# A hybrid decoder layer on one core: half of the output projection inside attention, later key queries inside the expert loop, and each expert row's diagonal made by ScalarE

## The chip, the cores and the metric

The kernel runs on 1 core of a Trainium2 chip. The metric is the device time of one execution in microseconds (us); the median of three runs is 1033.25 (1033.0 to 1033.98). Engines: TensorE (PE, matmuls; PEld its weight loads), VectorE (DVE), ScalarE (ACT), GpSimd (POOL) and SyncE (SP), which here only issues DMAs.

## The reference

Input x is 256 tokens of 1024 float32. One layer does this:

```python
z, xbc, dt, q, kvs, gate = split(h @ w_in)
y_ssd = rms_norm(ssd_scan(conv(xbc), dt) * silu(z))           # in 2 groups of 512
y_att = rms_norm(sparse_attention(q, kvs, gate))              # 16 heads, 3 branches
mix   = concatenate([y_ssd, y_att], -1) @ w_out
h     = layer_norm(ALPHA * h + mix)
# PEER: product-key retrieval, 8 heads, 16 experts of 16384 per head and token
s     = (h @ w_query) against sub_keys;  top 16 of each half, top 16 of their 256 sums
g     = softmax(chosen scores);  e = chosen expert numbers
a     = gelu(dot(h, expert_u[e]))
ffn   = sum over the 128 (head, k) of  g * a * expert_v[e]
out   = layer_norm(ALPHA * h + ffn)
```

The learned weight of rms_norm multiplies on, the scale of a token is one number per token.

## The kernel before, in words

Tokens stand on the 128 partitions, in two tiles (i = 0, 1). The program has a serial part and a loop.

Serial part: input projections of both tiles, convolution, SSD scan of both tiles, then attention of tile 0 (function calls `scores`, `maxima`, `exps`, `weights`, `weight_transposes`, `weight_copy`, `values`, in steps u of two heads, three ahead), its output projection (`mixer_transposes`, `mix_part`), residual and first layer norm, transposes of h (`hidden_transposes`), queries (`query_part`, `query_transposes`, `key_scores`) and the choice of the experts of head 0 (`choose`, all VectorE).

Loop: 256 rows, `g`, 128 per tile and 16 per head (`u = g // 16`, `k = g % 16`). For each row GpSimd gathers per partition one 8 KB line, the expert's u and v (1 MB in all), into a ring of 8 slots (10 from row `SWITCH` on, when the weights' buffers are free). VectorE dots its u half with h (L1514), ScalarE takes the gelu, VectorE multiplies the identity by gelu and gate into one of four diagonal matrices (`weigh`, L1486, one row later: `LAG`), and TensorE multiplies the diagonal by the v half, adding into two banks (`weighted`, L923, which signals `row_used` for GpSimd). VectorE also chooses the experts of the next head, in parts after rows 1 to 7 of a head.

Into the rows of tile 0, tile 1's attention, projection, norm and queries are threaded. A table written by hand (`step_tables`) says after which row each engine issues which piece; each engine runs its own list in order, and semaphores join them. SyncE brings 2 MB pieces of weights into two buffers, each asked for when the piece two before is used up; they share the DMA engines with the gathers. `bank_plan` deals the eight PSUM banks to the pieces in the same order.

## Time and profile before

| | us |
|---|---|
| median of three runs | 1033.25 |
| the profiled execution | 1033.95 |
| its span, first to last instruction | 1032.1 |
| busy: TensorE, weight loads | 890.0, 445.6 |
| busy: VectorE, ScalarE, GpSimd | 664.8, 267.7, 312.0 |
| mean granted TensorE clock | 0.969 |
| read from memory | 333.50 MB, of it 268.45 MB gathers |

Busy time is the sum of an engine's instructions, and says nothing of whether anyone waited for them. The DMA share is the mean busy share of the core's 16 DMA engines. "Idle before <-X" is the time in which an engine stood still ahead of an instruction, and what released it. A clock of 1.0 is TensorE's 2.4 GHz level, 0.5 its 1.2 GHz level; a value between is a mean over both.

### The profile page before, as it was taken

How to read it: one execution, taken by the hardware profiler on the slowest of the kernel's cores; microseconds unless marked ns; L12 is line 12 of the kernel's file. 1: busy time of each engine (PE TensorE's matmuls, PEld its weight loads, DVE VectorE, ACT ScalarE, POOL GpSimd, SP SyncE). 2: the span in 40 equal slices, each digit the busy share in tenths (PEclk: the TensorE clock that was granted, in tenths of full speed). 3: DMA queues.
4: the chain of work that ended last, by engine and by line, in shares of the span. 5: the costliest groups of instructions: out<-in, count | busy, mean ns of one | idle time of the engine just before them, and what ended most of it. 6: DMA issues, size and time to landing. Idle time of an engine off the chain costs nothing.

```text
span 1032.1 us, 8596 instructions
## 1 busy us (share of the span) xinstructions
PE 890.0 (86%) x2666; PEld 445.6 (43%) x2666; DVE 664.8 (64%) x1654; ACT 267.7 (26%) x665; POOL 312.0 (30%) x294
## 2 busy tenths in 40 slices
PE   7999998859788998998999888889888787877875
PEld 6876546546354343444544333344333222222221
DVE  2512005851243998989977685859879788788755
ACT  1121125373022555554321121113112011021000
POOL 0020001200030443443533343343535543444420
PEclk9999999989899898999999998989999999999998
DMA  6343664002659898999999999999999999999991
GB/s 252 147 140 141 231 263 174 1 1 82 244 208 423 340 422 326 407 388 377 396 421 423 422 421 422 421 422 399 399 421 421 421 421 422 420 422 421 420 422 64
DMA packets 44477, 335.11 MB, mean 325 GB/s; under 512 B 5904, under 2 KB 5904, under 8 KB 7824
## 3 DMA queue, kind: packets, MB, share of 16 engines
q0 software_dynamic: 36864, 268.45, 63.5%
q1 hardware_dynamic: 7568, 66.12, 16.4%
q8 instruction: 21, 0.34, 0.1%
q14 instruction: 24, 0.20, 0.0%
HBM read 333.50 MB, written 1.05 MB: 324 GB/s over the span
## 4 chain that ended last, share of the span: by engine, by line
PE 35%; DVE 23%; DMA 23%; issue 11%; ACT 7%; POOL 1%; DVEq 0%; SPq 0%; POOLq 0%; ACTq 0%
DMA late<-in_uv,eidx 11%; PE ps L649 8%; PE ps L923 7%; PE ps L641 6%; DMA ring<-in_uv,eidx 5%; DMA wring<-in_uv,eidx 5%; PE ps L784 5%; PE ps L758 4%; ACT L967 3%; DVE late L1514 3%; DVE late L1486 3%; ACT tmp L967 3%; DVE ring L1514 3%; DVE late L1194 2%; DMA wring<-in_wts 1%
## 5 line engine op out<-in xcount | busy, mean ns | idle before, releaser
L923 PE MATMUL ps<-late 128*128 128x512 f32 x480 | 233.2, 617 | 42.1 <-DVE late L1486 41.5
L923 PE MATMUL ps<-ring,late 128*128 128x512 f32 x480 | 234.7, 623 | 40.1 <-DVE late L1486 39.8
L1610 POOL DMA_INDIRECT late<-in_uv,eidx x120 | 134.6, 1122 | 294.6 <-PE ps L923 191.0
L1610 POOL DMA_INDIRECT ring<-in_uv,eidx x120 | 140.1, 1168 | 183.2 <-PE ps L923 179.8
L967 ACT ACTIVATE late<-late 128x1 f32<-128x1 f32 (+2 forms) x275 | 58.7, 218 | 511.2 <-DVE late L1514 510.4
L1514 DVE CUSTOM_DVE_ANT_0 late<-late,x_sb 128x1024 f32<-128x1024 f32 x120 | 146.7, 1223 | 56.6 <-DMA late<-in_uv,eidx 55.1
L1514 DVE CUSTOM_DVE_ANT_0 ring<-ring,x_sb 128x1024 f32<-128x1024 f32 x120 | 146.7, 1222 | 55.5 <-DMA ring<-in_uv,eidx 53.4
L923 PEld LDWEIGHTS ps<-ring,late 128*128 128x128 f32 x480 | 87.9, 196 | 162.5 <-DVE late L1486 83.2
L923 PEld LDWEIGHTS ps<-late 128*128 128x128 f32 x480 | 86.6, 194 | 163.7 <-DVE late L1486 88.0
L967 ACT ACT_TABLE_LOAD x84 | 107.8, 1283 | 14.5 <-PE ps L641 13.0
L1486 DVE TENSOR_SCALAR late<-cst,late 128x128 f32<-128x128 f32 x256 | 88.0, 344 | 26.7 <-ACT late L967 26.6
L649 PE MATMUL ps<-wring,tmp 128*128 128x347 f32 (+4 forms) x256 | 84.6, 492 | 0.0
L967 ACT ACTIVATE tmp<-ps 128x512 f32<-128x512 f32 (+3 forms) x88 | 44.4, 513 | 86.5 <-PE ps L641 41.2
L641 PE MATMUL ps<-tmp,wring 128*128 128x256 f32 x256 | 58.0, 391 | 6.7 <-DMA wring<-in_wts 6.7
L649 PEld LDWEIGHTS ps<-wring,tmp 128*128 128x128 f32 x256 | 48.5, 189 | 35.5 <-issue 14.8
L784 PE MATMUL ps<-wring,tmp 128*128 128x512 f32 (+1 forms) x144 | 58.8, 558 | 0.7 <-issue 0.7
L641 PEld LDWEIGHTS ps<-tmp,wring 128*128 128x128 f32 x256 | 50.4, 197 | 13.9 <-DMA wring<-in_wts 6.7
L923 PE MATMUL ps<-wring,late 128*128 128x512 f32 x64 | 31.4, 615 | 10.4 <-DVE late L1486 10.3
L784 PEld LDWEIGHTS ps<-wring,tmp 128*128 128x128 f32 x144 | 28.1, 198 | 27.6 <-issue 25.4
L1233 DVE TENSOR_SCALAR dtb<-dtb 128x32 f32<-128x32 f32 x1 | 0.2, 181 | 58.8 <-ACT dtb L967 58.8
L967 ACT ACTIVATE late<-ps 128x512 f32<-128x512 f32 (+4 forms) x22 | 11.5, 524 | 79.7 <-PE ps L649 74.2
L1584 POOL TENSOR_TENSOR tmp<-late,cst 128x128 f32<-128x128 f32 x4 | 1.8, 452 | 91.6 <-PE ps L659 91.4
(198 smaller groups left out, 822.7 us busy)
## 6 DMA issues: line engine op xcount, KB each, us to landing
wring<-in_wts SPq DMA_DIRECT2D x23, 2048.0 KB, 10.1
wring<-in_wts SPq DMA_DIRECT2D x2, 1428.0 KB, 5.7
wring<-in_wts SPq DMA_DIRECT2D x2, 1388.0 KB, 5.6
wring<-in_wts SPq DMA_DIRECT2D x4, 512.0 KB, 7.4
lnw<-in_ln SPq DMA_DIRECT2D x4, 512.0 KB
late<-in_uv,eidx POOLq DMA_INDIRECT x120
ring<-in_uv,eidx POOLq DMA_INDIRECT x120
wring<-in_wts SPq DMA_DIRECT2D x1, 1432.0 KB, 7.3
```

The costliest lines, as they stand in the source:

```text
L641: last = mm(o[:, 0:T], w[:, c % 4, k, :], xT_sb[:, k, :], start=k == 0, stop=k == KD - 1)
L649: last = mm(o[:, 0:width], xT_sb[:, k, i * P:(i + 1) * P], w[:, k, :], start=k == 0, stop=k == KD - 1)
L758: last = mm(mix[half], mixTs[i][n][:, c, :], mix[2][:, c, half * 512:(half + 1) * 512], start=m + c == 0, stop=n + c == 6)
L784: last = mm(o[:, 0:heads * 256], hTails[i][:, k, :], w[:, k, first * 256:(first + heads) * 256], start=k == 0, stop=k == KD - 1)
L923: last = mm(o[n], diag[:, g % DIAGS, :], v_row[:, n * 512:(n + 1) * 512], start=False, stop=False, skip_group_check=True)
L967: return nc.scalar.activation(out, in_, func, **kw)
L1194: return V.tensor_tensor(out, a, b, op)
L1233: link(V.tensor_scalar(dtb[:, 4, :, :], dtb[:, 2, :, :], 1.0, None, ALU.add))
L1486: V.tensor_scalar(diag[:, g % DIAGS, :], ident, wact[:, e, 0, k:k + 1], gate[:, e, k:k + 1], ALU.mult, ALU.mult).then_inc(diag_ready, 1)
L1514: V.tensor_tensor_reduce(out=u_row, in0=u_row, in1=h_sb[:, i, :], scale=1.0, scalar=0.0, op0=ALU.mult, op1=ALU.add, accum_out=hdot[:, e, k ...
L1584: G.tensor_tensor(krt[:, :, 0:HD // 2], src[:, :, HD // 2:HD], bc(ksin[:, 0:HD // 2], 1, NKV), ALU.mult)
L1610: G.indirect_dma_start(row(slots[g]), None, uv, bass.IndirectOffsetOnAxis(eidx[:, u % 2, k:k + 1], 0)).then_inc(row_here[slots[g]], 16)
```

## The change

It has five parts. (1) The gate multiply of the SSD output moves to the end of each tile's SSD scan, the squares of both tiles to the start of attention. TensorE transposes tile 0's SSD half at u = -1 and does its share of the output projection in eight slices, one after `values` of each step, into banks of its own (`mixS`); the attention half goes into `mixA`, and its rms scale, one number per token, is applied in the residual instead of ahead of the transposes. (2) Residual, layer norm and last output work in halves of 512 columns. (3) Only the queries of heads 0 to 3 stay ahead of row 0; heads 4 to 7 follow in the loop at rows 14, 25, 36 and 47 (`EARLY`). (4) `choose` has 15 small parts instead of 7, spread over rows 16u - 23 to 16u - 9; `SWITCH` is 160. (5) ScalarE makes gate times gelu and the diagonal, both as copies with a scale; the lag of a row is gone, as are the two matmul pairs with zeros that opened and closed a sum.

```diff
-SWITCH = 176
+SWITCH = 160
-LAG = 1
+EARLY = 3
...
+    for n, k in enumerate((14, 25, 36, 47)):
+        queries(0, EARLY + n, k, 1, 3)
...
# tensor
             for u in range(-AHEAD, NU[0] + 1):
...
+                if u == -1:
+                    mixer_transposes(0, 0)
                 if u >= 1:
                     values(0, u - 1)
+                    c = u - 1
+                    mix_blocks(0, c // 4, by_block[c % 4 * 2:c % 4 * 2 + 2])
...
-            mixer_transposes(0, 0)
-            for m in range(4):
-                mix_part(0, m)
             mixer_transposes(0, 1)
             for m in range(4, 8):
                 mix_part(0, m)
             hidden_transposes(0)
-            for n in range(len(QUERIES[0])):
+            for n in range(EARLY):
...
# scalar, in the loop
                 f(wact[:, e, 0, k:k + 1], hdot[:, e, k:k + 1], ACT.Gelu).then_inc(w_step, 1)
+                if k == 0:
+                    act.wait_ge(gate_ready, u + 1)
+                act.wait_ge(w_step, g + 1)
+                f(wact[:, e, 1, k:k + 1], wact[:, e, 0, k:k + 1], ACT.Copy, scale=gate[:, e, k:k + 1]).then_inc(gw_step, 1)
+                act.wait_ge(gw_step, g + 1)
+                if g >= DIAGS:
+                    act.wait_ge(row_used, g - DIAGS + 1)
+                f(diag[:, g % DIAGS, :], ident, ACT.Copy, scale=wact[:, e, 1, k:k + 1]).then_inc(diag_ready, 1)
...
# vector
-            def weigh(g):
-                dve.wait_ge(w_step, g + 1)
-                if g >= DIAGS:
-                    dve.wait_ge(row_used, g - DIAGS + 1)
-                V.tensor_scalar(diag[:, g % DIAGS, :], ident, wact[:, e, 0, k:k + 1], gate[:, e, k:k + 1], ALU.mult, ALU.mult).then_inc(diag_ready, 1)
...
+            def residual(i, half):
+                if half == 0:
+                    dve.wait_ge(sd_ready, 2 * i + 2)
+                    link(V.reciprocal(st[:, 12:13], st[:, 20:21]))
+                o = await_full(dve, "mixA", i, half)
+                cols = slice(half * 512, (half + 1) * 512)
+                taken(V.scalar_tensor_tensor(r1s[i][:, cols], o, st[:, 12:13], x_sb[:, i, cols], ALU.mult, ALU.add), "mixA", i, half)
+                await_taken(dve, "mixA", i, half)
+                statistics(r1s[i], half, 24)
+            def layer_norm(dst, src, scratch, at, value, ln_value, part, ready):
+                if part == 0:
+                    dve.wait_ge(ln_here, ln_value)
+                    for half in range(2):
+                        cols = slice(half * 512, (half + 1) * 512)
+                        last = V.scalar_tensor_tensor(scratch[:, cols], src[:, cols], bna[:, 0:1], lnw[:, 0, cols], ALU.subtract, ALU.mult)
+                    link(last)
+                else:
+                    dve.wait_ge(sd_ready, value)
+                    link(V.reciprocal(st[:, at:at + 1], st[:, at + 8:at + 9]))
+                    for half in range(2):
+                        cols = slice(half * 512, (half + 1) * 512)
+                        V.scalar_tensor_tensor(dst[:, cols], scratch[:, cols], st[:, at:at + 1], lnw[:, 1, cols], ALU.mult, ALU.add).then_inc(ready, 1)
```

TensorE before, from the last steps of tile 0's attention on (L867 transposes of the weights, L880 and L889 values, L746 transposes for the projection, L758 the projection, L769 transposes of h):

```order
L867 MATMUL ps<-cst,tmp 128x128 x4
L880 MATMUL ps<-late,tmp 128x256
L889 MATMUL ps<-late,tmp 128x64 x8
L746 MATMUL ps<-cst,s_all 128x128 x8
L758 MATMUL ps<-wring,late 128x512 x16
L746 MATMUL ps<-cst,s_all 128x128 x8
L758 MATMUL ps<-wring,late 128x512 x16
L769 MATMUL ps<-cst,x_sb 128x128 x8
```

TensorE after, at the same place (L896, L909 and L918, L767, L778 and L798 are those lines' new numbers):

```order
L896 MATMUL ps<-cst,tmp 128x128 x4
L909 MATMUL ps<-late,tmp 128x256
L918 MATMUL ps<-late,tmp 128x64 x4
L778 MATMUL ps<-wring,late 128x512 x2
L918 MATMUL ps<-late,tmp 128x64 x4
L778 MATMUL ps<-wring,late 128x512 x2
L767 MATMUL ps<-cst,s_all 128x128 x8
L778 MATMUL ps<-wring,late 128x512 x16
L798 MATMUL ps<-cst,x_sb 128x128 x8
```

The first projection of 16 matmuls is gone from behind the last values, and pairs of its matmuls stand behind the values of each step instead.

ScalarE before, near row 5 to 10 of the loop (late 128x1 is the gelu, tmp,lsum the exponentials of tile 1's attention; their table loads stand between):

```order
L967 ACT_TABLE_LOAD
L967 ACTIVATE tmp,lsum<-ps,nmx 128x256 x2
L967 ACT_TABLE_LOAD
L967 ACTIVATE late<-late 128x1 x3
L967 ACT_TABLE_LOAD
L967 ACTIVATE tmp,lsum<-ps,nmx 128x256 x2
L967 ACT_TABLE_LOAD
L967 ACTIVATE late<-late 128x1 x3
L967 ACTIVATE tmp<-ps 128x512
L967 ACTIVATE late<-late 128x1
L967 ACTIVATE tmp<-ps 128x512
```

ScalarE after, at the same place (late<-late 128x1 x2 is a gelu and the product with the gate, late<-cst,late the diagonal):

```order
L992 ACT_TABLE_LOAD
L992 ACTIVATE tmp,lsum<-ps,nmx 128x256 x2
L992 ACT_TABLE_LOAD
L992 ACTIVATE late<-late 128x1 x2
L992 ACTIVATE late<-cst,late 128x128
L992 ACTIVATE late<-late 128x1 x2
L992 ACTIVATE late<-cst,late 128x128
L992 ACTIVATE late<-late 128x1 x2
L992 ACTIVATE late<-cst,late 128x128
```

Every gelu is followed by its product and its diagonal, and the exponentials of a unit stand between the diagonals of two rows.

TensorE after, inside the loop where the first late query stands (L953 a row's matmuls, L813 the query's, L888 and L889 scores, L909 and L918 values of tile 1); before, no L784 stands among the rows ahead of row 98:

```order
L953 MATMUL ps<-ring,late 128x512 x4
L909 MATMUL ps<-late,tmp 128x256
L918 MATMUL ps<-late,tmp 128x64 x4
L813 MATMUL ps<-wring,tmp 128x256 x4
L953 MATMUL ps<-ring,late 128x512 x2
L888 MATMUL ps<-kT,tmp 128x512
L889 MATMUL ps<-cmask_h,ident_h 128x2x128
L813 MATMUL ps<-wring,tmp 128x256 x4
L953 MATMUL ps<-late 128x512 x2
```

The query's 8 matmuls come in two parts of four between the rows.

## Rows read from the trace of the kernel before

**Rows 1.** Busy us (xcount) per engine by stretch; granted clock, DMA share, GB/s.

```profile
196.93:241.04 44.11, 30.64 (x174) 23.26 (x173) 21.91 (x53) 29.73 (x98) 7.19 (x12) 0.88 0.00 1
299.55:329.72 30.17, 25.04 (x84) 12.12 (x83) 5.00 (x15) 6.95 (x12) 8.21 (x8) 1.00 0.95 390
329.72:499.71 169.99, 161.19 (x513) 77.22 (x513) 151.08 (x398) 88.68 (x190) 71.01 (x60) 0.95 0.95 378
499.71:740.00 240.29, 216.41 (x528) 95.23 (x526) 184.32 (x470) 46.83 (x126) 95.50 (x84) 0.96 1.01 416
740.00:1008.00 268.00, 210.97 (x450) 77.97 (x451) 209.65 (x533) 40.85 (x133) 118.31 (x104) 1.00 1.01 421
```

**Rows 2.** GpSimd in order: start, duration, gather [idle before <-releaser].

```profile
299.55 1.14 POOL L1610 DMA_INDIRECT late<-in_uv,eidx  x1 [93.75 <-DVE eidx L1394]
...
329.72 1.48 POOL L1610 DMA_INDIRECT late<-in_uv,eidx  x1 [19.83 <-PE ps L923]
```

**Rows 3.** TensorE in order, from attention of tile 0 to the queries.

```profile
208.76 0.63 PE L867 MATMUL ps<-cst,tmp 128*128 128x128 f32 x4 [3.77 <-ACT tmp L967]
...
241.04 1.04 PE L746 MATMUL ps<-cst,s_all 128*128 128x128 f32 x8
...
258.56 13.97 PE L758 MATMUL ps<-wring,late 128*128 128x512 f32 x32 [0.44 <-DVE late L1194]
...
281.70 5.26 PE L784 MATMUL ps<-wring,tmp 128*128 128x256 f32 x16 [0.73 <-issue]
...
288.92 3.62 PE L784 MATMUL ps<-wring,tmp 128*128 128x256 f32 x16
...
303.60 1.13 PE L801 MATMUL ps<-sk,tmp 128*128 128x128 f32 x8 [0.73 <-issue]
```

**Rows 4.** VectorE in order: residual, layer norm, dot of row 0.

```profile
271.78 1.48 DVE L1339 SCALAR_TENSOR_TENSOR late<-x_sb,ps 128x512 f32<-128x512 f32 x2 [12.63 <-PE ps L758]
...
277.72 1.22 DVE L1194 TENSOR_TENSOR x_sb<-late,lnw 128x1024 f32<-128x1024 f32 x1
...
305.37 1.23 DVE L1514 CUSTOM_DVE_ANT_0 late<-late,x_sb 128x1024 f32<-128x1024 f32 x1 [5.77 <-DMA late<-in_uv,eidx]
```

**Rows 5.** DMA issues of the page: xcount, KB each, us to landing.

```profile
wring<-in_wts SPq DMA_DIRECT2D x23, 2048.0 KB, 10.1
```

**Rows 6.** Groups in 329.72 to 499.71: busy, mean ns, idle before <-releaser.

```profile
L923 PE MATMUL ps<-ring,late 128*128 128x512 f32 x118 | 58.6, 624 | 5.8 <-DVE late L1486 5.8
...
L1486 DVE TENSOR_SCALAR late<-cst,late 128x128 f32<-128x128 f32 x61 | 21.1, 345 | 14.6 <-ACT late L967 14.6
```

**Rows 7.** ScalarE's groups in 329.72 to 499.71.

```profile
L967 ACT ACT_TABLE_LOAD x40 | 51.3, 1283 | 0.7
...
L967 ACT ACTIVATE late<-late 128x1 f32<-128x1 f32 x61 | 11.4, 200 | 82.2 <-DVE late L1514 81.8
L967 ACT ACTIVATE tmp<-ps 128x512 f32<-128x512 f32 x16 | 9.3, 579 | 0.0
```

**Rows 8.** ScalarE's 128x128 group in attention of tile 0.

```profile
L967 ACT ACTIVATE tmp<-ps,nmx 128x128 f32<-128x128 f32 x32 | 11.3, 382 | 3.1 <-DVE nmx L1429 3.0
```

**Rows 9.** ScalarE in order inside the loop.

```profile
409.79 0.58 ACT L967 ACTIVATE tmp<-ps 128x512 f32<-128x512 f32 x1
410.39 1.28 ACT L967 ACT_TABLE_LOAD   x1
411.69 0.47 ACT L967 ACTIVATE tmp<-ps,nmx 128x256 f32<-128x256 f32 x1
```

**Rows 10.** All engines in order, the tail.

```profile
1015.42 1.23 DVE L1514 CUSTOM_DVE_ANT_0 ring<-ring,x_sb 128x1024 f32<-128x1024 f32 x1 [0.98 <-DMA ring<-in_uv,eidx]
...
1016.97 3.70 PE L923 MATMUL ps<-ring,late 128*128 128x512 f32 x8 [0.49 <-DVE late L1486]
...
1021.57 0.69 DVE L1492 SCALAR_TENSOR_TENSOR tmp<-x_sb,ps 128x512 f32<-128x512 f32 x1 [4.29 <-PE ps L960]
...
1028.76 0.34 SPq L616 DMA_DIRECT2D out<-tmp  x1
```

More of the change, by code:

```diff
@@ L97, in step_tables @@
     put("pe", 8, "pcT")
[L98 removed]
+    put("act", 11, "pcT")
     for u in range(NU[1]):
@@ L135, in step_tables, with queries @@
-    for n, k in enumerate((130, 131, 133, 134, 137, 138, 139)):
-        put("dve", k, "finish", n)
-    put("act", 135, "root2")
-    return at
+    def queries(i, n, k, gap, copy):
+        for part in range(2):
+            put("pe", k + part * gap, "q", i, n, part)
+        k += gap
+        put("act", k + copy, "q", i, n)
+        put("pe", k + copy + 1, "qpT", i, n)
+        put("act", k + 2 * copy + 1, "qpT", i, n)
+        put("pe", k + 2 * copy + 2, "s", i, n)
+        put("act", k + 3 * copy + 2, "s", i, n)
@@ new lines, in step_tables @@
+    for n, k in enumerate((14, 25, 36, 47)):
+        queries(0, EARLY + n, k, 1, 3)
+    put("pe", 60, "mT", 0)
+    put("dve", 63, "mT", 0)
+    for part, k in enumerate((64, 67, 69, 71)):
+        put("pe", k, "mix", part)
+    put("dve", 70, "taken")
+    put("act", 71, "squares")
+    put("pe", 72, "mT", 1)
+    put("dve", 73, "mean")
+    put("act", 74, "root", 12, 4)
+    for half in range(2):
+        put("dve", 74 + half, "partial", half)
+    put("dve", 76, "mT", 1)
+    for part, k in enumerate((77, 79, 81, 83)):
+        put("pe", k, "mix", 4 + part)
@@ new lines, in step_tables, with choice_step @@
+    put("dve", 85, "residual", 0)
+    put("dve", 87, "residual", 1)
+    put("act", 88, "root", 24, 5)
+    put("dve", 88, "norm", 0)
+    put("dve", 89, "norm", 1)
+    put("pe", 90, "hT")
+    put("act", 93, "hT")
+    queries(1, 0, 94, 2, 3)
+    queries(1, 1, 108, 4, 4)
+    queries(1, 2, 126, 4, 4)
+    queries(1, 3, 144, 4, 4)
+    for part, k in enumerate((132, 133, 135, 136)):
+        put("dve", k, "finish", part)
+    put("act", 134, "root", 36, 6)
+    return at
+def choice_step(u, part):
+    if u == 1:
+        return part // 2
+    if u == PH:
+        return TOPK * u - 21 + max(part - 2, 0)
+    return TOPK * u - 23 + part
@@ L554, in layer @@
         for i in range(NT):
-            order += [(14 + n, 3 * i + n + 1 if n < 3 else ("mix", i, 1)) for n in range(4)]
+            order += [(14 + n, (2 * i + 1, ("mixS", i, 1), 2 * i + 2, ("mixA", i, 1))[n]) for n in range(4)]
             order += [(18 + n, ("q", i, max(g for g, group in enumerate(QUERIES[i]) if group[0] == n))) for n in range(4)]
@@ L913, in _ @@
             hidden_transposes(0)
-            for n in range(len(QUERIES[0])):
+            for n in range(EARLY):
                 query_part(0, n, 0, 1)
@@ L931, in _ @@
                 o = [await_free(pe, "y", i, n) for n in range(2)]
-                for n in range(2):
-                    mm(o[n], zero, nothing, start=True, stop=False, skip_group_check=True)
                 for g in range(STEPS * i, STEPS * (i + 1)):
                     weighted(g, o)
-                    for what, n in items_at["pe"][g]:
+                    for what, *n in items_at["pe"][g]:
                         if what == "compressed":
@@ L1124, in _ @@
             token_copies(0)
+            for i in range(NT):
+                ssd_squares(i)
             compressed_exp(0)
+            root(0, 2 * NG, 1)
             for u in range(-AHEAD, NU[0]):
@@ L1464, in _ @@
                     maxima(0, u + AHEAD)
-                if u in GATE_AT:
-                    ssd_gate(GATE_AT.index(u))
-                if u - 1 in GATE_AT:
-                    ssd_norm(GATE_AT.index(u - 1))
+                if u == 0:
+                    mixer_transposed(0, 0)
+                if u == 1:
+                    ssd_norm(1)
             attention_taken(0)
-            mixer_transposed(0, 0)
+            mixer_transposed(0, 1)
+            for half in range(2):
+                partial(0, half)
```

412 lines of the change are left out of this document (180 added, 232 removed).

## The prediction

> **What bounds the kernel now.** Read first the busy time by stretch [rows 1]: mean GB/s and DMA share there say where the memory queue is full. From 499.71 us on it is: 416 GB/s, then 421, at a DMA share of 1.01. That is the ceiling of this loop; each of its 256 rows is a 1 MB gather (2.49 us at 421 GB/s), and nothing that an engine saves there moves the end. Three parts lie outside that ceiling. Before 299.55 us the gathers have not begun. From 299.55 to 329.72 (390 GB/s) and on to 499.71 (378 GB/s) the queue has gaps: the two stretches moved 30.17 x 390 + 169.99 x 378 = 76,020 KB (GB/s times us), which at 421 are 180.6 us, but took 200.2. So 19.6 us are lost there. Last comes the tail behind the last row.
>
> Next, GpSimd's own rows [rows 2]. Eight gathers go out from 299.55, when the first indices are ready; the ninth waits 19.83 us for TensorE and goes at 329.72. From there to the 69th at 499.71, where I cut the stretch, there are 60 rows (x60 for GpSimd in its row, [rows 1]) in 170.0 us, 2.83 us each, slower than the queue. In that stretch TensorE is busy 161.19 of 169.99 us at a clock of 0.95, VectorE 151.08, ScalarE 88.68: TensorE is the nearest to a bound, with VectorE close behind, and the ring starts it 20 us in arrears.
>
> Then the path to 299.55 on TensorE and VectorE [rows 3, 4]. Attention of the first tile ends at 241.04; behind it stand in a row the output projection of the SSD half and that of the attention half, 13.97 us each with transposes ahead (the second, from 258.56, stands for both), residual and layer norm, transposes, and queries from 281.70. In 196.93 to 241.04 TensorE worked only 30.64 of 44.11 us [rows 1].
>
> **The change, part by part.**
>
> *First gather.* The SSD half of the projection (16 matmuls, 13.97 us) and its 8 transposes (1.04 us) move into attention. TensorE's work there becomes 30.64 + 13.97 + 1.04 = 45.65 us, more than the 44.11 us the stretch has now, so TensorE becomes its bound. Some idle time stays: the first weights to be transposed appear at 208.76, after a wait of 3.77 and a shorter one; I keep 5 us. The clock, 0.88 on average in this stretch, should be nearer to full without the later pauses; I take 2 us back (of at most 30.64 x 0.12 = 3.7). The gate multiply of tile 0 (a 1024-wide VectorE operation, 1.22 us by [rows 4]) now stands in the SSD stage ahead of the second tile's work and delays the start by 1.2. End of attention with its mixing: 196.93 + 1.2 + 45.65 - 2 + 5 = 246.8. Transposes of the attention half: 1.2 with the first copy behind them, so the projection runs 248.0 to 262.0; its scale is applied only in the residual, hence no norm ahead of it. VectorE then does half a residual (0.74), its statistics (as wide, 0.7), small ones (0.4), two half-width multiplies (1.3), a reciprocal and two more (1.5): 4.8 with gaps, to 266.8. One transposing group and its copy remain: 268.1, where queries start, against 281.70. The choice behind it has the same instructions. So the first gather moves by 13.6, to 286.0. Were all the old idle time (13.5) to stay, it would be 294; with 2 us of idle and the whole clock, 281. A 2 MB piece of weights lands in 10.1 us at the median [rows 5]; the last of w_out is asked for when the SSD half is done (246.8) and needed 7 us into the attention half, at 255: this could cost 2, which is inside these bounds.
>
> *First 60 rows.* Queries of heads 4 to 7 leave the stretch ahead of row 0. TensorE is free at 304.73 - 13.6 = 291.1 [rows 3]; row 0 is dotted 5.8 us after its issue, as now, at 291.8. Then dot 1.3, three ScalarE operations 0.9, two matmuls 2.0: row 0 is used at 296.0 and the ninth gather goes at 296.1, 10.1 us after the first instead of 30.2. The ring no longer runs dry at the start. What those queries cost inside the loop: four groups of one head, each 8 matmuls of 256 columns (3.62 by [rows 3]) with transposes and scores, about 4.3 together: 17.2 us on TensorE, in rows 14 to 60. The stretch for 60 rows is then 161.19 + 17.2 = 178.4 plus idle. Idle was 8.8, 5.8 of it waits for VectorE's diagonal before the one kind of row alone [rows 6]. VectorE loses 60 x 0.34 us of diagonals and 14.6 us of waits for ScalarE, and can run ahead by as many rows as the ring holds, so I take half, 4.5 (bounds 0 and 20). The 69th gather goes at 296.1 + 183 = 479.1. The same 180.6 us of transfers lie ahead of it, so the gaps are 479.1 - 286.0 - 180.6 = 12.5 us instead of 19.6: 7.1 gained. With no idle and the clock full (161.19 x 0.95 + 17.2 = 170) they are 0 by this sum; 3 stay for the first landing. With 20 of idle they are 28.
>
> *ScalarE.* No operation of it in the trace multiplies by a per-row scalar onto 128 columns. The nearest row is the 128x128 exponential with a pointer bias, 382 ns; above it stands 579 for 512 columns and below it 200 for one column [rows 7, 8]. I take 0.38, and 0.20 for the product of gate and activation, as for the gelu. Each waits for the one before it. Per row: 0.20 + 0.38 and 0.08 of handing over more than now. In the stretch: 88.68 + 60 x 0.66 + 12 copies x 0.38 = 133 us of 183. It fits on average. It also shortens the path from a row's landing to its use by most of a row, since VectorE made each diagonal one row late; beyond row 68 the full queue hides that, and it shows in the tail alone. The copies need no table: in the row at 409.79 a copy runs between a gelu and the load for exp [rows 9], and the list of instructions has 80 loads against 84.
>
> The Trainium skill (ScalarE: Activation LUTs, What ACT_TABLE_LOAD costs) says that a switch costs a load of about 1283 ns and a drain of about 1380 ns behind it. The load agrees; the drain does not show here: the load at 410.39 is followed by the exponential at 411.69, 1.30 us on.
>
> *Finer choice, earlier tenth slot.* The same instructions in fifteen parts; indices of the next head are ready at the same rows (16u - 10, and row 118 for head 8). Where the queue is full this is worth nothing; if heads were late it would show at row 128, and 499.71 to 740 loses only 240.3 x 5/421 = 2.9 us. The ring of ten from row 160 instead of 176 lies in that full queue: nothing.
>
> *Tail.* Now: last dot at 1015.42, the matmuls of the last two rows from 1016.97 (3.70), a closing matmul pair, first residual at 1021.57, output issued at 1028.76 [rows 10]. After: dot 1.2, ScalarE 0.9, one row's matmuls 2.0, so the residual starts 4.2 us after the dot instead of 6.15; from there 2.8 for residual and statistics, 0.5 small ones, 1.3 and 1.5 for the norm with the last half issued 6.2 later instead of 7.2, and half a transfer, 0.3 less. Together 3.2 gained (bounds 2 and 4).
>
> **Sum**, against the profiled execution's own 1033.95 us (span 1032.1): -13.6 - 7.1 - 3.2 = -23.9, so 1010.0; the median of the runs lies 0.7 lower, hence **1009.3**, say 1009.
>
> **Rivals.**
> *The queue never starves after the first row.* For: eight rows of lead are kept, and VectorE is relieved. Against: 178 us of TensorE work for 60 rows is more than their 149 us of gathers, and close to the 180.6 of all transfers. Gaps 3 instead of 12.5: 1000.
> *ScalarE is late now and then.* Its order is fixed: a unit of attention puts two table loads (2.57) and two exponentials between two rows' diagonals, and four diagonals are all the lead it has. For: VectorE already waited 14.6 us there for gelus behind such loads [rows 6], and now TensorE stands directly behind them. Against: 73% busy. With 20 us of idle on TensorE: 1025. If every one of the 40 loads of the stretch [rows 7] cost 1.38 more, ScalarE's own work would be 188 us, the stretch 5 longer than TensorE's 183 and with its waits 9: 1018. That is what the drain of the Trainium skill's rule (same page and section) would do; the rows speak against it.
> *TensorE stays as interrupted in attention as before.* The first gather at 294 instead of 286: 1017.
> *Slower than before.* ScalarE becomes the bound of the first 60 rows: a diagonal waits for a slot that TensorE frees, TensorE for a value unit's copy that stands behind that diagonal. The gain of 24 us is used up when 60 rows take 183 + 24 = 207 us, 3.45 each; ScalarE's work is 2.2 of it, so 1.25 of waiting per row is the turning point. At 3.6 per row the time is 1042. Against: the copies stand three steps behind the matmuls they need.
>
> **How the numbers follow.** A difference under 0.2% (2 us) can't be told from none. Forecast 60%, with its own range 1003 to 1015; never starving 17%; ScalarE late 10%; the drain 2%; attention as before 5%; slower 5%; everything cancelling out 1%. The range goes from below the case without starvation with an early first gather (281: -5) and a tenth cut off, to between attention as before and ScalarE late: 997 to 1021. Faster 0.94, same 0.01, slower 0.05.
>
> **What would show it.** First gather at 286 (281 to 290) and ninth within 11 us of it; TensorE busy over 43 us from 197 to 247; the 69th gather at 479 and about 390 GB/s between; from there 416 to 421 as before; no more waits of VectorE on ScalarE; the operation with 128 columns on ScalarE at 0.38; residual 4.2 us behind the last dot. I am wrong if TensorE's waits for ScalarE's diagonal in these 60 rows pass 10 us, if the first gather is later than 290, or if the full queue after row 68 falls below 415.

## The result, and the profile after

The changed kernel takes **1006.07 us** (median of 4 runs, 1003.62 to 1006.71) against 1033.62 us (1033.0 to 1035.21, 4 runs) before: 0.9727 of it, 95% interval 0.9707 to 0.9747. 1009 was predicted, with 997 to 1021 as the range. The profiled execution of the changed kernel took 1003.62 us with a span of 1001.8; it is the fastest of the four, 2.5 us under their median, so the traces differ by 30.3 us where the medians differ by 27.6.

First the busy times by stretch, in the columns of [rows 1]. Cuts are at the first gather (287.51), the ninth (299.85), the 69th (473.81), rows 128 and 200, and the start of the last dot (988.57):

```profile
196.93:247.97 51.04, 44.81 (x225) 29.27 (x225) 25.14 (x57) 29.86 (x99) 7.25 (x12) 0.97 0.13 46
...
287.51:299.85 12.34, 7.80 (x23) 3.48 (x21) 2.51 (x9) 3.98 (x7) 8.04 (x9) 0.79 0.85 335
299.85:473.81 173.96, 172.90 (x597) 92.63 (x597) 140.12 (x360) 132.33 (x327) 65.97 (x61) 0.96 1.00 408
473.81:654.43 180.62, 161.59 (x397) 71.52 (x396) 114.00 (x274) 75.95 (x211) 65.89 (x61) 0.95 1.01 422
654.43:828.82 174.39, 149.04 (x343) 59.30 (x341) 126.35 (x312) 80.09 (x234) 76.92 (x73) 0.99 1.01 421
828.82:988.57 159.75, 126.02 (x253) 44.78 (x254) 98.27 (x218) 66.04 (x202) 54.69 (x56) 0.98 0.97 404
```

Against [rows 1] the reader sees three things. TensorE, at 161.19 of 169.99 us in the 60 rows before, is now busy 172.90 of 173.96. VectorE fell from 151.08 to 140.12, ScalarE rose from 88.68 to 132.33. And the queue, at 390 and 378 GB/s from the first gather to the 69th before, now runs at 335 and 408. The short first stretch has the landing of the first row in it. Both together are 12.34 x 335 + 173.96 x 408 = 75,110 KB, which are 178.4 us at 421 GB/s and took 186.3: 7.9 us of gaps, against 19.6. The forecast had set the same 180.6 us of transfers ahead of the 69th gather; it is 2.2 less, and those 2.2 us come behind it.

GpSimd's first gather and its ninth, which answer to [rows 2]:

```profile
287.51 1.15 POOL L1632 DMA_INDIRECT late<-in_uv,eidx  x1 [77.35 <-DVE eidx L1444]
...
299.85 0.94 POOL L1632 DMA_INDIRECT late<-in_uv,eidx  x1 [2.17 <-PE ps L953]
```

The wait of 19.83 us in front of the ninth is 2.17 now.

TensorE in order, answering to [rows 3]; L778 is the projection, L767 and L798 transposes, L813 queries, L953 a row's matmuls:

```profile
244.72 1.94 PE L778 MATMUL ps<-wring,late 128*128 128x512 f32 x4
246.50 1.04 PE L767 MATMUL ps<-cst,s_all 128*128 128x128 f32 x8
247.97 13.97 PE L778 MATMUL ps<-wring,late 128*128 128x512 f32 x32 [0.44 <-DVE late L1219]
266.25 1.48 PE L798 MATMUL ps<-cst,x_sb 128*128 128x128 f32 x8 [4.31 <-DVE x_sb L1305]
268.46 6.48 PE L813 MATMUL ps<-wring,tmp 128*128 128x256 f32 x16 [0.73 <-issue]
...
295.82 3.75 PE L953 MATMUL ps<-late 128*128 128x512 f32 x4 [3.12 <-ACT late L992]
```

One projection stands behind attention now, and queries start at 268.46 instead of 281.70.

Row 0 on ScalarE and VectorE (an x2 of 128x1 is gelu and product, the 128x128 the diagonal):

```profile
293.17 1.23 DVE L1540 CUSTOM_DVE_ANT_0 late<-late,x_sb 128x1024 f32<-128x1024 f32 x1 [5.60 <-DMA late<-in_uv,eidx]
293.36 1.28 ACT L992 ACT_TABLE_LOAD   x1
...
294.65 0.59 ACT L992 ACTIVATE late<-late 128x1 f32<-128x1 f32 x2
...
295.28 0.40 ACT L992 ACTIVATE late<-cst,late 128x128 f32<-128x128 f32 x1
```

The groups in 299.85 to 473.81 that answer to [rows 6, 7]:

```profile
L953 PE MATMUL ps<-ring,late 128*128 128x512 f32 x116 | 54.7, 597 | 1.1 <-ACT late L992 1.1
L992 ACT ACT_TABLE_LOAD x38 | 48.8, 1283 | 0.7
...
L992 ACT ACTIVATE late<-late 128x1 f32<-128x1 f32 x126 | 31.2, 248 | 26.0 <-DVE late L1540 23.5
...
L992 ACT ACTIVATE late<-cst,late 128x128 f32<-128x128 f32 x62 | 25.0, 404 | 2.0
```

The 5.8 us of TensorE's waits are 1.1, and ScalarE's waits for VectorE's dots fell from 81.8 in 32 times to 23.5 in 14: most gelus now find their dot done. Among VectorE's waits there is none for a gelu any more.

The tail, all engines in order, against [rows 10]:

```profile
988.57 1.23 DVE L1540 CUSTOM_DVE_ANT_0 late<-late,x_sb 128x1024 f32<-128x1024 f32 x1 [1.24 <-DMA late<-in_uv,eidx]
...
989.83 0.54 ACT L992 ACTIVATE late<-late 128x1 f32<-128x1 f32 x2 [1.51 <-DVE late L1540]
990.40 0.40 ACT L992 ACTIVATE late<-cst,late 128x128 f32<-128x128 f32 x1
...
990.86 1.98 PE L953 MATMUL ps<-late 128*128 128x512 f32 x4 [0.49 <-ACT late L992]
...
992.88 0.69 DVE L1530 SCALAR_TENSOR_TENSOR tmp<-x_sb,ps 128x512 f32<-128x512 f32 x1 [3.08 <-PE ps L953]
...
998.38 0.99 SPq L634 DMA_DIRECT2D out<-tmp  x2
```

One row's matmuls instead of two rows' stand behind the last dot, and the residual starts 4.31 us behind it instead of 6.15.

In this table the span is cut at four events; the sum of the column "difference" is the difference of the spans.

| stretch | before, us | after, us | difference | predicted |
|---|---|---|---|---|
| start to first gather | 299.55 | 287.51 | -12.04 | -13.6 |
| first to 69th gather | 200.16 | 186.30 | -13.86 | -7.1 |
| 69th gather to last dot | 515.71 | 514.76 | -0.95 | 0 |
| last dot to the end | 16.68 | 13.23 | -3.45 | -3.2 |

The middle two, -14.8 together, are for the most part the gaps (-11.7) and the 2.9 us that [rows 1] lost between 499.71 and 740.00 (416 GB/s); from the 69th gather to row 200 (828.82) the queue now runs at 422 and 421.

### The profile page after: what moved, and what is told of

The parts are those of the page before. It is cut to its first block, busy times and chain, and to the rows that moved or that the text cites. A ratio compares the mean times of both kernels' runs of the same rounds, so it can differ in the third digit from the quotient of the medians.

```text
span 1001.8 us, 8992 instructions
## 1 busy us (share of the span) xinstructions
PE 883.1 (88%) x2680; PEld 449.2 (45%) x2682; DVE 590.4 (59%) x1401; ACT 440.6 (44%) x1178; POOL 290.5 (29%) x294
## 4 chain that ended last, share of the span: by engine, by line
PE 50%; DMA 33%; DVE 9%; ACT 5%; issue 2%; POOL 1%; DVEq 0%; SPq 0%; POOLq 0%; ACTq 0%
PE ps L953 19%; DMA ring<-in_uv,eidx 13%; DMA late<-in_uv,eidx 12%; PE ps L667 8%; DMA wring<-in_uv,eidx 6%; PE ps L659 6%; PE ps L778 4%; PE ps L813 4%; ACT late L992 2%; PE ps L918 2%; DVE ring L1540 2%; DVE late L1540 2%; ACT L992 2%; DMA wring<-in_wts 1%; PE ps L888 1%
## 5 line engine op out<-in xcount | busy, mean ns | idle before, releaser
L992 ACT ACTIVATE late<-late 128x1 f32<-128x1 f32 (+1 forms) x531 | 135.7, 256 | 310.8 <-DVE late L1540 300.0
L953 PE MATMUL ps<-ring,late 128*128 128x512 f32 x464 | 227.9, 620 | 42.0 <-ACT late L992 41.9
L953 PE MATMUL ps<-late 128*128 128x512 f32 x480 | 235.3, 624 | 30.4 <-ACT late L992 30.4
L1632 POOL DMA_INDIRECT late<-in_uv,eidx x120 | 128.5, 1071 | 266.4 <-PE ps L953 182.8
L1632 POOL DMA_INDIRECT ring<-in_uv,eidx x116 | 122.2, 1054 | 194.5 <-PE ps L953 186.7
L953 PEld LDWEIGHTS ps<-late 128*128 128x128 f32 x480 | 88.8, 197 | 149.5 <-issue 82.8
L953 PEld LDWEIGHTS ps<-ring,late 128*128 128x128 f32 x464 | 83.8, 194 | 160.5 <-ACT late L992 86.8
L992 ACT ACTIVATE late<-cst,late 128x128 f32<-128x128 f32 x256 | 103.2, 403 | 10.8 <-PE ps L953 2.6
L667 PEld LDWEIGHTS ps<-wring,tmp 128*128 128x128 f32 x256 | 48.5, 189 | 35.5 <-issue 14.8
L813 PE MATMUL ps<-wring,tmp 128*128 128x256 f32 (+1 forms) x176 | 61.1, 496 | 0.7 <-issue 0.7
L992 ACT ACTIVATE late<-ps 128x512 f32<-128x512 f32 (+5 forms) x30 | 14.6, 488 | 82.1 <-PE ps L667 74.2
L953 PE MATMUL ps<-wring,late 128*128 128x512 f32 x80 | 40.3, 631 | 10.4 <-ACT late L992 10.4
L813 PEld LDWEIGHTS ps<-wring,tmp 128*128 128x128 f32 x176 | 34.7, 202 | 23.0 <-issue 19.1
L1540 DVE CUSTOM_DVE_ANT_0 wring<-wring,x_sb 128x1024 f32<-128x1024 f32 x20 | 24.5, 1226 | 17.5 <-DMA wring<-in_uv,eidx 17.5
## 6 DMA issues: line engine op xcount, KB each, us to landing
lnw<-in_ln SPq DMA_DIRECT2D x4, 512.0 KB, 12.5
```

The source lines that it names most:

```text
L667: last = mm(o[:, 0:width], xT_sb[:, k, i * P:(i + 1) * P], w[:, k, :], start=k == 0, stop=k == KD - 1)
L813: last = mm(o[:, 0:heads * 256], hTails[i][:, k, :], w[:, k, first * 256:(first + heads) * 256], start=k == 0, stop=k == KD - 1)
L953: last = mm(o[n], diag[:, g % DIAGS, :], v_row[:, n * 512:(n + 1) * 512], start=g % STEPS == 0, stop=(g + 1) % STEPS == 0, skip_group_chec ...
L992: return nc.scalar.activation(out, in_, func, **kw)
L1540: V.tensor_tensor_reduce(out=u_row, in0=u_row, in1=h_sb[:, i, :], scale=1.0, scalar=0.0, op0=ALU.mult, op1=ALU.add, accum_out=hdot[:, e, k ...
L1632: G.indirect_dma_start(row(slots[g]), None, uv, bass.IndirectOffsetOnAxis(eidx[:, u % 2, k:k + 1], 0)).then_inc(row_here[slots[g]], 16)
```

## The experiments

All ratios are to the kernel before, on the same chip; its median there was 1033.5 to 1033.8 us. Differences from the changed kernel are taken between medians of separate comparisons, where the changed kernel's own interval is 2 us either way, so one or two microseconds between them mean nothing. "60 rows" means from the ninth gather to the 69th in the profiled execution. Theory: 13.6 us come from the SSD half of the projection inside attention, 7 from the queries in the loop and the relieved VectorE, 3 from the tail.

**The diagonal back on VectorE.** The dot of a row is followed by the diagonal of the row before it; all else is as after.

```diff
+LAG = 1
...
-                f(wact[:, e, 1, k:k + 1], wact[:, e, 0, k:k + 1], ACT.Copy, scale=gate[:, e, k:k + 1]).then_inc(gw_step, 1)
-                f(diag[:, g % DIAGS, :], ident, ACT.Copy, scale=wact[:, e, 1, k:k + 1]).then_inc(diag_ready, 1)
...
+                if g >= LAG:
+                    weigh(g - LAG)
```

> The changed kernel with part 5 undone: VectorE makes the diagonal again, one row late, with gate and gelu in one 0.34 us operation. Mine (first gather, TensorE's work in the first 60 rows, tail): the first gather stays at 287.5; in the next 60 rows VectorE gets 20 us more on 140 of 174 and stays below TensorE's 173, so the gaps in the gathers grow by 0 to 4; the tail gets about 1.5 to 2 longer. About 1010 us against 1006. Rival (VectorE was the bound of these rows, and its relief the main gain): the rows go back to 2.83 us each, the 69th gather to about 487, 1018 us or more.

Measured: 1014.52 us, 0.9812 [0.9787, 0.9837], 8.5 us over the changed kernel. The ninth gather came 19.9 us after the first instead of 12.3, and the reason for that stands in the order of VectorE and TensorE (a group of matmuls with its wait in brackets):

```profile
301.15 1.23 DVE L1543 CUSTOM_DVE_ANT_0 late<-late,x_sb 128x1024 f32<-128x1024 f32 x1 [5.86 <-DMA late<-in_uv,eidx]
...
302.30 0.34 DVE L1526 TENSOR_SCALAR late<-cst,late 128x128 f32<-128x128 f32 x1
...
302.79 3.75 PE L954 MATMUL ps<-late 128*128 128x512 f32 x4 [10.73 <-DVE late L1526]
```

Row 0 had its dot at 292.74, but its diagonal stood behind row 1's dot, and row 1 landed later. With the queries out of the way, TensorE waits 10.7 us here, 7.6 more than in the changed kernel. Its 60 rows:

```profile
306.82:478.11 171.29, 170.92 (x596) 92.00 (x596) 149.40 (x400) 90.40 (x199) 72.24 (x60) 0.97 0.98 392
```

TensorE has no idle time to speak of in them, and they are 2.7 us shorter than the changed kernel's; VectorE waits for a gelu 7.0 us in all. In the profiled execution, 10.5 us longer than the changed kernel's, the first gather comes 0.6 earlier, the 69th comes 4.9 later counted from the first, the stretch from there to the last dot is 5.2 longer (519.98 against 514.76; what makes those 5.2 isn't shown), and the tail 1.0. So part 5 is worth 8.5 us on top of the others, where I had expected about 4.

**The SSD half's 16 matmuls behind attention again**, its scale and norms staying as changed.

```diff
-                    c = u - 1
-                    mix_blocks(0, c // 4, by_block[c % 4 * 2:c % 4 * 2 + 2])
...
+            for m in range(4):
+                mix_part(0, m)
             mixer_transposes(0, 1)
```

> The changed kernel with the SSD half's 16 projection matmuls behind attention again, in one block (13.97 us); its transposes and the gate stay where the change put them. Mine: attention of tile 0 ends earlier by some 6 to 10 us, since TensorE has less to do there, but the block follows it, so the first gather comes 8 to 12 us later than 287.5 only by what was idle time; everything behind moves along: 1014 to 1018. Rival (what is lost ahead of the loop is won back in it, because weights are loaded by then): 1009 or less.

Measured: 1005.52 us, 0.9726 [0.971, 0.9742]: no difference from the changed kernel, and the expectation failed. The order on TensorE shows why; the two long rows are the two halves of the projection:

```profile
234.13 13.95 PE L778 MATMUL ps<-wring,late 128*128 128x512 f32 x32
247.92 1.04 PE L767 MATMUL ps<-cst,s_all 128*128 128x128 f32 x8
249.40 13.97 PE L778 MATMUL ps<-wring,late 128*128 128x512 f32 x32 [0.44 <-DVE late L1219]
```

Attention's values end at 234.1 here, 12.4 us earlier than the values with their pairs in the changed kernel (246.50). So of the 14 us of matmuls some 2 at most had filled idle time, and the rest had pushed attention back. The same stretch, 196.93 to 235.00, in the changed kernel and then here says it as well: TensorE is busy 33.58 with the pairs and 31.51 without, so the pairs had filled 2.1 of its idle time by then.

```profile
196.93:235.00 38.07, 33.58 (x162) 21.80 (x162) 23.01 (x53) 24.33 (x89) 7.25 (x12) 0.96 0.13 46
```

```profile
196.93:235.00 38.07, 31.51 (x195) 23.49 (x196) 24.69 (x56) 28.69 (x97) 7.25 (x12) 0.96 0.00 1
```

The projection's second half starts 1.4 us later here, and the first gather goes at 288.94 instead of 287.51. Hiding the SSD half is worth 1.4 us at most, once the norm no longer interrupts attention. The pairs alone in the kernel before, with its 13.5 us of idle time left in place, were not run.

**The kernel before, with the gate, the squares, one root and the norm of the SSD half moved out of attention's steps** (the other half of what I had taken for one edit).

```diff
-                if u in GATE_AT:
-                    ssd_gate(GATE_AT.index(u))
-                if u - 1 in GATE_AT:
-                    ssd_norm(GATE_AT.index(u - 1))
...
+            for i in range(NT):
+                ssd_squares(i)
+            act.wait_ge(ms_ready, 2)
+            f(st[:, 8:12], st[:, 4:8], ACT.Sqrt).then_inc(sd_ready, 2)
```

> The kernel before with one thing moved: gate multiply of each tile at the end of its SSD scan, squares of both tiles ahead of attention, one root for both, norm of tile 0 early. The output projection stays behind attention, all queries ahead of the rows, diagonal on VectorE. New theory (the 12 us of the first gather are for the larger part the removed waits of attention for the root and its table loads, not the 14 us of projection put into it): attention of tile 0 ends at about 234 to 235 instead of 241, first gather at 293 to 294, all behind it as before: about 1027 us. Rival (the projection inside attention does it): 1032 or more, first gather 298 or later.

Measured: 1024.56 us, 0.9917 [0.9902, 0.9933]: -8.9 us; 1027 had been expected. The first gather moves from 299.55 to 290.53:

```profile
290.53 1.14 POOL L1615 DMA_INDIRECT late<-in_uv,eidx  x1 [79.87 <-DVE eidx L1398]
```

Next to nothing behind it changes: from it to the last dot 715.5 us against 715.9, tail 16.65 against 16.68. The waits of the kernel before in 196.93 to 241.04 name what went (total, times, longest), then its table loads there, and those of this experiment:

```profile
PE ps L867 <- DVE tmp L1194: 8.6, 3, 5.2
...
DVE st L1265 <- ACT st L967: 6.3, 2, 3.2
DVE st L1263 <- ACT ring L967: 3.1, 2, 2.1
```

```profile
L967 ACT ACT_TABLE_LOAD x4 | 5.1, 1283 | 0.1
```

```profile
L967 ACT ACT_TABLE_LOAD x2 | 2.6, 1283 | 0.1
```

VectorE stood 9.4 us in waits for ScalarE's squares and roots (1.7 are left in this experiment), each root between two table loads, and what TensorE had to transpose (tmp, L1194) queued behind them.

The 60 rows of this experiment answer another question, what bounds them in the kernel before:

```profile
320.70:491.03 170.33, 158.47 (x513) 75.61 (x513) 151.42 (x398) 88.68 (x190) 70.04 (x60) 0.97 0.96 377
```

TensorE worked 2.7 us less than in [rows 1] (158.47 against 161.19, at a granted clock of 0.97 against 0.95), and the rows took as long, 170.33 us against 169.99. All the waits that the profile shows for it there are for VectorE's diagonals, and they grew from 8.7 to 11.7 us, while VectorE has shown waits for gelus alone, 14.6 in both (before, then here):

```profile
PE ps L923 <- DVE late L1486: 8.7, 13, 1.8
```

```profile
PE ps L923 <- DVE late L1491: 11.7, 15, 1.9
```

VectorE's 151.08 us of work and 14.6 of waits are 165.7 of the 170.0. So the bound of these rows was VectorE with its waits for ScalarE, and TensorE, with more work, followed it.

**Queries back ahead of the loop.**

```diff
-QUERIES = [[(0, 0, 1), (0, 1, 1), (1, 0, 2), (2, 0, 1), (2, 1, 1), (3, 0, 1), (3, 1, 1)], [(n, 0, 2) for n in range(4)]]
-EARLY = 3
+QUERIES = [[(0, 0, 1), (0, 1, 1), (1, 0, 2), (2, 0, 2), (3, 0, 2)], [(n, 0, 2) for n in range(4)]]
+EARLY = 5
...
-for n, k in enumerate((14, 25, 36, 47)):
+for n, k in enumerate(()):
```

> The changed kernel with all queries of tile 0 ahead of row 0, as before. Mine: first gather unchanged at 287.5, ninth at about 318 instead of 300; then TensorE has 17 us less to do in 60 rows (about 163 us), 69th gather at about 481 instead of 474; gaps about 13 instead of 8: 1011. Rival (TensorE is the bound, so taking 17 us from it inside the rows pays): 1003 or less.

Measured: 1011.71 us, 0.9789 [0.9773, 0.9806], as expected: 5.6 us slower. The ninth gather came 32.5 us after the first; the 60 rows took 157.4 us instead of 174.0. The 20 us that the ring gains at the start are for the most part paid back by the same matmuls inside it.

**The choice in seven parts and the ring of ten from row 176, as before.**

```diff
-SWITCH = 160
+SWITCH = 176
...
-CHOOSE_STEPS = [2, 2, 2, 2, 2, 1, 2, 1, 1, 1, 2, 1, 1, 1, 1]
+CHOOSE_STEPS = [5, 5, 3, 3, 3, 2, 1]
...
-    if u == 1:
-        return part // 2
-    if u == PH:
-        return TOPK * u - 21 + max(part - 2, 0)
-    return TOPK * u - 23 + part
+    return TOPK * (u - 1) + 1 + part
...
```

> The changed kernel with the choice in seven parts after rows 1 to 7 again, and slots nine and ten from row 176. Mine: both lie where the DMA queue is full or TensorE is the bound: 1006, within 1. Rival (coarse parts hold up the maxima of tile 1's attention and the rows behind them): about 3 us in gaps, 1009.

Measured: 1006.73 us, 0.974 [0.9724, 0.9757]. Nothing, as expected.

**Part 5 alone, in the kernel before.**

```diff
+                f(wact[:, e, 1, k:k + 1], wact[:, e, 0, k:k + 1], ACT.Copy, scale=gate[:, e, k:k + 1]).then_inc(gw_step, 1)
+                f(diag[:, g % DIAGS, :], ident, ACT.Copy, scale=wact[:, e, 1, k:k + 1]).then_inc(diag_ready, 1)
...
-                if g >= LAG:
-                    weigh(g - LAG)
```

> The kernel before with part 5 alone: ScalarE makes product and diagonal, no lag. Mine: TensorE's 8.8 us of waits in the stretch of 60 rows shrink to about 1 to 2, the tail by about 1.5: 1033.6 - 7 - 1.5 = about 1025. First and ninth gather as before (299.6, 330). Rival 1 (relief is worth nothing while the ring starts 20 us in arrears): 1032. Rival 2 (ScalarE in its fixed order holds up TensorE): 1036 or more.

Measured: 1018.64 us, 0.985 [0.9834, 0.9867]: -15.0 us against the 1033.62 of the result (-15.2 against the same chip's 1033.8), nearly twice what I had given it. Its 60 rows, in the columns of [rows 1]:

```profile
331.50:491.04 159.54, 155.26 (x513) 76.07 (x513) 131.70 (x323) 129.26 (x313) 71.30 (x60) 0.97 0.99 403
```

The same 513 matmul records as in [rows 1] take 155.26 us instead of 161.19, and the rows 159.5 instead of 170.0. Of the 5.9 us less work some 3 go with the granted clock, 0.97 against 0.95; the norm experiment had the same clock, 2.7 us less work and no gain from it. In the kernel before VectorE waited for gelus, by this row of its waits between 299.55 and 499.71:

```profile
DVE late L1486 <- ACT late L967: 26.6, 10, 12.1
```

These are gone. The longest of them was no loss, though: it is VectorE's first diagonal of the loop, and the gelu for it stood on ScalarE behind copies for the last queries.

```profile
327.06 0.34 DVE L1486 TENSOR_SCALAR late<-cst,late 128x128 f32<-128x128 f32 x1 [12.07 <-ACT late L967]
```

TensorE was at work on those queries and the opening pairs with zeros until 326.60 anyhow, and with part 5 alone the ninth gather comes no earlier (30.6 us after the first, 30.2 before). The other nine waits, 14.6 us, stand in the 60 rows, and with them VectorE's 21.1 us of diagonals leave the engine that was their bound. Of the 14.2 us between the two spans 10.5 arise in these rows, 1.0 in the tail and 4.6 between the 69th gather and the last dot (511.15 us against 515.71), while the first gather is 1.3 later and the ninth 0.4 more. The gaps from the ninth gather on are 6.8 us here, 17.4 before. Both traces have 84 table loads, so product and diagonal on ScalarE brought none.

**ScalarE with a second, unused diagonal in every row; VectorE with an unused 128x128 multiply in every row.**

```diff
+                f(spare[:, :], ident, ACT.Copy, scale=wact[:, e, 1, k:k + 1])
```

> The changed kernel with a second, unused diagonal per row on ScalarE (0.40 us more a row, 24 us in the first 60 rows on 132 of 174, 0.4 on the way from a row's landing to its use). Mine: ScalarE has room, and the full queue hides the delay: tail +0.4, gaps +0 to 3: 1006.5 to 1009. Rival (ScalarE is close to being the bound of the first rows): gaps +8 or more, 1014.

```diff
+                link(V.tensor_scalar(spare[:, :], ident, 1.0, 0.5, ALU.mult, ALU.mult))
```

> The changed kernel with an unused 128x128 VectorE operation after every dot, waited for (about 0.4 us a row, as much as the diagonal that the change took from it), everything else unchanged. Mine: VectorE stays below TensorE, gaps +0 to 3: 1006 to 1009. Rival (VectorE's relief is the main gain): 1014 or more.

Measured: 1006.08 us, 0.9734 [0.9718, 0.975], with ScalarE; 1010.59 us, 0.9775 [0.9758, 0.9791], with VectorE. The 60 rows of the two:

```profile
300.59:476.05 175.46, 172.38 (x596) 92.62 (x596) 139.24 (x357) 148.88 (x387) 67.84 (x60) 0.96 0.99 403
```

```profile
301.31:478.60 177.29, 173.23 (x596) 92.70 (x596) 153.58 (x419) 131.68 (x325) 61.94 (x60) 0.96 0.99 400
```

ScalarE at 148.88 of 175.46 us costs nothing. The added operation on VectorE takes 223 ns and is waited for once a row; it costs 4.5 us over the run, where 62 of them take 13.8 us in the stretch. It is only two thirds of the 345 ns that the change took from VectorE [rows 6], and still the time lies 1.6 us above the expected range. So VectorE's own load matters, with the engine 80% busy, and ScalarE had room for more than it got. By proportion, an estimate, 345 ns a row would cost 7.0 us, which is near the 8.5 that the first experiment gave: how much of part 5's worth is VectorE's load and how much its waits and its lag isn't separated by these runs. The profiled execution is 7.0 us longer than the changed kernel's: the first gather is 1.5 later, the 69th counted from the first 3.3, the last dot counted from the 69th 2.2. The ninth comes 12.3 us after the first, as in the changed kernel, where with VectorE's diagonal it was 19.9: the late first row is the lag's doing, not the load's.

**VectorE's diagonal in its own row, without the lag of one** (the first experiment with LAG = 0).

```diff
-LAG = 1
+LAG = 0
```

> e1 (changed kernel, VectorE makes the diagonal) without the lag of a row: VectorE waits for the gelu and makes the diagonal of the row it has just dotted. Theory: of the 8.5 us that e1 cost, the late ninth gather (19.9 us after the first instead of 12.3) and 1 us of the tail come from the lag and go, but VectorE now stands 0.3 us per row for the gelu and longer behind ScalarE's table loads: 1008 to 1012. Rival A (it is all the lag): 1006. Rival B (VectorE's waits for ScalarE are what hurts): 1020 or more.

Measured: 1038.02 us, 1.0045 [1.003, 1.0061]: slower than before the change, and far from what was expected. VectorE's largest wait over the whole run, and its 60 rows:

```profile
DVE late L1526 <- ACT late L993: 99.1, 241, 2.1
```

```profile
299.35:503.52 204.17, 181.08 (x596) 94.85 (x596) 156.54 (x408) 89.62 (x198) 64.74 (x60) 0.95 0.91 355
```

The early start is kept (ninth gather 12.2 us behind the first), but 241 rows make VectorE stand still for a gelu, 0.4 us each at the mean and 2.1 at the longest. With the changed kernel's engine for the same diagonal the wait isn't there. So VectorE can have the early first row or nearly no waits (7.0 us with the lag of one), not both; ScalarE has both, because there the product and the diagonal follow the gelu on one engine.

**Four query groups ahead instead of three**, the loop's three at rows 25, 36, 47; then the same at rows 38, 49, 58.

```diff
-EARLY = 3
+EARLY = 4
...
-for n, k in enumerate((14, 25, 36, 47)):
+for n, k in enumerate((25, 36, 47)):
```

> The changed kernel with head 4's query also ahead of row 0 (four groups ahead, three in the rows). TensorE now stands idle 3.1 us before row 0 and then runs 10 us at the lower clock. Mine: its 4.3 us of work fills that pause; the ninth gather comes about 1 later or not at all, and 4.3 us less stand in the rows: gaps 8 to about 4: 1002 to 1004. Rival (the ninth gather decides): it comes 4 later and the time is 1008 to 1010.

> e7 (four query groups ahead of row 0) with the other three at rows 38, 49 and 58 instead of 25, 36 and 47. Theory: TensorE's arrears are largest before row 60, and work that comes later in them is covered by the rows in the ring; 4.3 us move behind row 60: 999 to 1001. Rival (the same work in the same 60 rows, only its order changed; or late scores hold up the choice of heads 5 to 7): 1002 or more.

Measured: 1001.77 us, 0.9687 [0.9671, 0.9703], and 1002.55 us, 0.9701 [0.9688, 0.9714]. The two can't be told apart; both are about 4 us faster than the changed kernel, and the best versions run here (the interval of the second just touches the changed kernel's). The first came out as expected in time but not in its steps: the ninth gather was to be 1 us later at most and is 5.4 later, and TensorE still waits 2.90 us before row 0. The second missed its 999 to 1001; its rival, the same work in the same rows in another order, fits. The 60 rows of both:

```profile
305.35:474.75 169.40, 168.48 (x574) 89.02 (x574) 136.59 (x348) 130.16 (x319) 67.57 (x60) 0.95 0.99 405
```

```profile
305.69:471.01 165.32, 162.89 (x568) 84.45 (x567) 137.29 (x352) 130.49 (x320) 67.96 (x61) 0.99 1.01 417
```

The group moved ahead costs its 5.4 us once, before the ninth gather, and frees TensorE in the stretch where it is the bound (busy 168.48 of 169.40 us). Whether the later rows keep the 0.99 of granted clock in every run isn't shown by one profile each.

## Why the prediction was right, and where its steps were not

The sum was right: -23.9 predicted, -27.6 by the medians, -30.3 by the profiled executions that it was worked out on. Some of it is luck: against those, the first two points below came 3.7 us too early in the forecast and the third 9.0 too late. And one reading ahead of the sum was wrong: "TensorE is the nearest to a bound" in the 60 rows before. Busy time alone says so, but the norm experiment shows VectorE with its waits for gelus as the bound there. Point by point:

- **First gather, 286.0 predicted, 287.51 measured. The step on "the SSD half of the projection moves into attention" named the wrong source.** It took 13.97 + 1.04 us of work as filling idle time that would otherwise stay. By the second experiment that filling is worth at most 1.4. Most of the gain, 9.0, is the idle time itself going away with the waits for squares, roots and their table loads, whether or not matmuls take its place (the norm experiment, which moves this work and its waits together). The residual and norm in halves give 2.6 by the rows, without an experiment of their own: queries start 6.5 us behind the projection's end (247.97 + 13.97) instead of 9.2. That attention with its pairs ended at 246.5, where 246.8 had been worked out, so confirms the sum of its work and not the reason for the gain: without the pairs it ends at 234.1. I had worked out one time from all of them and named the first as its source. TensorE in 196.93 to 247.97 was busy 44.81 of 51.04 us, over the 43 given as a sign: that sign doesn't tell the two sources apart, and shouldn't have been used for it. Of the missing 1.5 us the first queries took 1.2: 6.48 us for the 5.26 of [rows 3], at a granted clock of 0.59 from 268.46 to 275.41 (0.70 from 281.70 to 287.00 before).
- **Ninth gather, 10.1 us after the first predicted, 12.3 measured.** Row 0's dot and diagonal came as worked out (ready 8.2 us after the first gather, 8.0 by the sum), but its four matmuls took 3.75 us instead of 2.0. From 295.82 to 299.50 the granted clock is 0.50, which is the 1.2 GHz level; TensorE had waited 3.12 us for the diagonal ahead of them.
- **The 60 rows, 183 us predicted, 174.0 measured; this is the mis-sized term.** TensorE's own work was 172.9, not 178.4: the 161.19 of [rows 1] was taken over as fixed, but the same matmuls take 155.3 to 158.5 us in the two experiments on the kernel before, at a granted clock of 0.97 instead of 0.95, and 156.3 us in the changed kernel with all queries ahead of the loop. It is as low without part 5 (170.92 with the queries in the rows and VectorE's diagonal, 172.90 with ScalarE's), so it isn't part 5's doing; why the work shrinks beyond the clock stays open. Its idle time was 1.1, not 4.5; half of 8.8 had been kept without a row for it. Gaps are 7.9 instead of the 12.5 predicted. The price of VectorE's waits was seen ([rows 6], 14.6 us) but entered only as relief of an engine that wasn't held to be the bound, and in the kernel before it was. By itself part 5 is worth 15.0 us, on top of the other parts 8.5; the other parts are worth 19.1 without it. What both would repair overlaps by 6.5.
- **ScalarE.** The diagonal took 404 ns, 0.38 had been taken from [rows 8]. The product is longer than the 0.20 taken: the 126 operations of 128x1 have a mean of 248 ns, so a pair takes 0.50 and the product 0.30 of it. 62 of either come to 43.6 us; ScalarE has 43.7 more than before (132.33 against 88.68), with 2.5 less in table loads and as much more in other work. 133 was predicted, of a longer stretch. The Trainium skill (ScalarE: Activation LUTs, What ACT_TABLE_LOAD costs) gives an operation 186 ns, 93 for a pointer operand and 0.833 per column. That is an estimate of 386 ns for the diagonal, 4% under the measured 404, and of 280 for the product, against the 0.30 us worked out here.
- **The full queue** ran at 421 to 422 GB/s as said. The 2.9 us that [rows 1] lost in it went too, which I had not predicted. Between rows 128 and 200 the loss is 2.8 before, 2.0 with the norm moved alone and 2.4 with VectorE's diagonal in its own row, but 0.6 or less in every other experiment profiled, with part 5 alone and with all but part 5. Which wait makes it stays open.
- **The tail**, 3.2 predicted, 3.45 measured, by the steps named. With VectorE's diagonal it was 1.0 longer.
- **The rivals.** The ring that never starves was the nearest of them to what happened (gaps 3, time 1000): its gaps were to be 3, the forecast's 12.5, and 7.9 came out. ScalarE being late did not happen, even with 16 us more work on it in the stretch. The one that ends slower than before, a wait turning the gain around, does exist, but on the other engine: VectorE waiting for ScalarE in its own row, 1038 us.

## What to carry to other kernels

When one engine's in-order stream waits for another engine again and again, moving the dependent operations onto the engine that makes their input can be worth more than their duration suggests: here it took 21.1 us of work and 14.6 of waits off VectorE in 60 rows, and 15 us off the kernel. To see which engine bounds a stretch, ask whose waits are for whom and add an engine's waits to its work: the busiest engine, TensorE, was only following. Before crediting a gain to work hidden in idle time, ask what made the idle time; if the change removes that too, the two must be priced apart, and a busy share alone will not separate them. Where one engine bounds a stretch, how much work to defer into it has to be tried: three groups of queries in the loop were better than four and better than none; one and two were not run.

## What the runs showed of the hardware

Stretches of the changed kernel, in the columns of [rows 1] (the granted clock is the third from the end):

```profile
268.46:275.41 6.95, 6.48 (x16) 4.90 (x16) 0.00 (x0) 0.39 (x1) 0.00 (x0) 0.59 0.00 0
...
295.82:299.50 3.68, 3.67 (x4) 1.14 (x4) 0.00 (x0) 0.00 (x0) 1.56 (x2) 0.50 1.01 427
299.50:306.44 6.94, 6.94 (x33) 6.90 (x33) 4.18 (x14) 1.29 (x5) 0.94 (x1) 0.50 0.99 414
```

- The first row's four 128x512 matmuls took 3.60 to 3.75 us wherever TensorE had just waited longer: 2.90 us with four query groups ahead, 3.12 in the changed kernel, 10.73 with VectorE's diagonal. They took 1.98 behind a wait of 0.86 in the kernel before, and of 0.49 in the tail of the changed kernel. The lower level lasted through the following group too: 299.50 to 306.44 has a granted clock of 0.50. So the 10.6 us from 295.82 on hold work of 5.3 at the upper level, and the loss is larger than the wait of 3.12 ahead of it. No experiment takes the wait alone away.
- The first queries ran at a granted clock of 0.59. Ahead of them, from 262.00 to 268.46, TensorE had been busy 1.47 of 6.46 us, with waits of 4.31 and then 0.73 us, at a granted clock of 0.91.
- A copy on ScalarE with a per-row scale needs no table of its own: 38 loads in the 60 rows of the changed kernel, with 62 gelus, products and diagonals between them, and over the whole trace 84 loads before and with part 5 alone, 80 in the changed kernel with ScalarE's diagonal and with VectorE's. An operation directly behind a load starts 1.29 us after the load did (293.36, then 294.65).
- An unused operation of 0.22 us on VectorE per row cost 4.5 us over 256 rows, although VectorE was idle 20% of the first 60 rows; on ScalarE one of 0.39 us cost nothing that could be measured.
